# A hybrid decoder layer on one core: routing in another order, two embedding jobs moved behind the last expert, one expert's weights loaded earlier

## What is computed

```
x1 = LN1(alpha*x + merged @ w_o)
lg = x1 @ w_rg + b_rg ; g = argmax(lg)              # expert group
le = (x1 @ w_re + b_re)[group g] ; top 2, softmax    # two experts a token
y  = sum over the two: weight * (silu(x1 @ w_gate[e]) * (x1 @ w_up[e])) @ w_down[e]
x2 = LN2(alpha*x1 + y)
x3 = LN3(alpha*x2 + sigmoid(x2 @ w_ple_gate + b) * (p @ w_ple))
```

## Time and profile before

| | |
|---|---|
| three runs | 579.6 us median, 578.49 to 579.79 |
| profiled execution | 579.29 us, span 577.6 us, mean granted TensorE clock 0.971 |
| TensorE products | busy 534.0 us, 92% of the span |
| VectorE | 291.0 us, 50% |
| ScalarE | 189.5 us, 33% |
| GpSimd | 65.5 us, 11% |
| HBM read and written | 150.43 MB and 2.90 MB, 265 GB/s over the span |
| chain that ended last | TensorE 66%, VectorE 13%, DMA 11%, ScalarE 3% |

### The profile page before, as it was taken

How to read it: one execution, slowest core, us unless ns; L and a number is a source line. 1 busy time by engine, 2 the same in 40 slices (tenths; PEclk the granted TensorE clock), 3 DMA queues, 4 the chain that set the end, 5 groups by cost and what they waited for, 6 DMA issues and landing times.

```text
span 577.6 us, 9625 instructions
## 1 busy us (share of the span) xinstructions
PE 534.0 (92%) x3647; PEld 386.8 (67%) x3647; DVE 291.0 (50%) x633; ACT 189.5 (33%) x357; POOL 65.5 (11%) x92
## 2 busy tenths in 40 slices
PE   7899979999999879988999999999998899969992
PEld 7899868888889878777574544544544445446871
DVE  3442776565485567678453223222222222368878
ACT  4445444434355333052331111111111111246333
POOL 2000002322260640000000000000000000014010
PEclk9999989999999998977999999999999999979997
DMA  8996434875240980078399999999999999990101
GB/s 277 371 348 200 133 119 136 289 232 172 86 147 19 306 302 14 1 291 364 130 422 337 424 421 423 421 422 421 421 422 422 422 419 422 386 328 30 56 37 54
DMA packets 48796, 153.72 MB, mean 266 GB/s; under 512 B 3376, under 2 KB 28149, under 8 KB 36336
## 3 DMA queue, kind: packets, MB, share of 16 engines
q1 hardware_dynamic: 43778, 138.25, 62.6%
q0 software_dynamic: 3936, 12.60, 7.0%
q10 hardware_dynamic: 1046, 2.37, 1.2%
HBM read 150.43 MB, written 2.90 MB: 265 GB/s over the span
## 4 chain that ended last, share of the span: by engine, by line
PE 66%; DVE 13%; DMA 11%; ACT 3%; issue 2%; POOL 2%; SPq 1%; DVEq 1%; ACTq 0%; POOLq 0%
PE bank L1948 17%; PE bank L1629 16%; DMA ring<-in_w_up_dram 8%; PE bank L1961 7%; PE bank L1589 6%; DMA ring<-in_w_in_dram 3%; PE bank L1817 2%; PE bank L1970 2%; PE bank L2056 2%; PE bank L1892 2%; PE bank L1684 1%; PE bank L1954 1%; PE bank L1859 1%; ACT arena L699 1%; DVE arena L1174 1%
## 5 line engine op out<-in xcount | busy, mean ns | idle before, releaser
L1948 PE MATMUL bank<-ring,arena 128*64 128x256 f32 x1024 | 128.6, 392 | 5.2 <-DMA ring<-in_w_up_dram 2.6
L1948 PEld LDWEIGHTS bank<-ring,arena 128*64 128x64 f32 x1024 | 70.0, 134 | 60.1 <-issue 21.1
L1336 DVE TENSOR_TENSOR arena<-bank,arena 128x512 f32 x32 | 22.1, 692 | 133.5 <-PE bank L1970 127.7
L1629 PE MATMUL bank<-x_high,w_high 128*128 128x320 f32 x248 | 79.8, 322 | 2.3 <-ACT arena L661 2.3
L1629 PE MATMUL bank<-x_low,w_high 128*128 128x320 f32 x248 | 77.3, 312 | 0.0
L1629 PE MATMUL bank<-x_high,w_low 128*128 128x320 f32 x248 | 77.1, 311 | 0.0
L1961 PE MATMUL bank<-ring,arena 128*64 128x512 f32 x256 | 61.9, 604 | 0.0
L972 DVE TENSOR_TENSOR w_low<-ring,w_high 128x1024 fp32r<-128x1024 f32 x32 | 40.1, 1259 | 27.8 <-ACT w_high L643 27.7
L1629 PEld LDWEIGHTS bank<-x_high,w_high 128*128 128x128 f32 x248 | 47.2, 190 | 4.0 <-issue 3.9
L1629 PEld LDWEIGHTS bank<-x_low,w_high 128*128 128x128 f32 x248 | 47.2, 190 | 0.1
L1629 PEld LDWEIGHTS bank<-x_high,w_low 128*128 128x128 f32 x248 | 47.2, 190 | 0.0
(11 more groups left out here) (317 smaller groups left out, 887.3 us busy)
## 6 DMA issues: line engine op xcount, KB each, us to landing
ring<-in_w_gate_dram SPq DMA_DIRECT2D x32, 1024.0 KB, 16.2
ring<-in_w_up_dram SPq DMA_DIRECT2D x32, 1024.0 KB, 18.4
ring<-in_w_down_dram SPq DMA_DIRECT2D x32, 1024.0 KB, 18.9
ring<-in_w_in_dram SPq DMA_DIRECT2D x16, 1024.0 KB, 10.9
arena<-in_cache_k_dram POOLq DMA_DIRECT2D x16, 256.0 KB, 3.8
arena<-in_cache_v_dram POOLq DMA_DIRECT2D x16, 256.0 KB, 3.8
ring<-in_w_o_dram SPq DMA_DIRECT2D x4, 1024.0 KB, 11.3
ring<-in_w_ple_gate_dram SPq DMA_DIRECT2D x4, 1024.0 KB, 16.5
```

Source lines behind the costliest of these rows:

```text
L1336: V.tensor_tensor(YsT[:, :, bass.ds(place, WIN)].rearrange("p (d c) n -> p c d n", d=2), b[:, :].rearrange("p (c d n) -> p c d n", c=4, d= ...
L1629: last = mm(bank[j % 2][:, 0:T], w[:, j % 4, k, :], x[:, k, :], start=(k == n == 0), stop=(k == KD - 1 and n == 2))
L1948: last = mm(b[WIN * f:WIN * (f + 1), 0:256].rearrange("p (s n) -> p s n", s=2), x[:, WIN * k:WIN * (k + 1)], w[:, :, k, f, :], start=(k == ...
```

## The change

Four things are done, and they touch all engines' lists.

Loads: SyncE issues the third expert's gate and up (`load_pair(2)`) behind the first's and ahead of the second's. GpSimd issues `x_again`'s sample rows and `ln1_side[0]` behind the eight adds, not ahead of them.

Routing: the second tile is turned ahead of the first tile's routing products, the third tile ahead of the embeddings' turn. ScalarE copies both halves of the second tile (VectorE's copy falls away), and casts `x_part[0]` before. VectorE's `part_low(1)` is earlier; the last `x_part` is made in two halves, one on either side of the permutation. The products for offset and count go behind the gather, five products on `ones` stand in their old place, and VectorE picks the first window before it reads the offsets.

Embeddings: job two moves from the expert loop (which is one loop now, not two) to the routing, jobs three and four from ahead of the last four experts to behind the last turned result, in other banks.

Last result: `pairs(4)` stays ahead of the last `put`, `low_gate(0)` goes behind it, `low_gate(1)` to GpSimd, and `low_gate(2)` two steps earlier in the turning.

```diff
-        EMBED_BANKS = (3, 4, 6, 7, 6)
-        EMBED_FIRST = 2
+        EMBED_BANKS = (3, 4, 5, 0, 2)
+        EMBED_FIRST = 3
-        GATE_POOL = (3, 5, 7)
+        GATE_POOL = (1, 3, 5, 7)
@@ sync
             load_pair(0)
+            load_pair(2)
             for e in range(1, 5):
-                load_pair(e)
+                if e != 2:
+                    load_pair(e)
                 load_down(e - 1)
@@ gpsimd
             pool.dma_start(x_again[:, 0:2, :], xp_d).then_inc(x2_here, 16)
-            for h in range(2):
-                pool.dma_start(x_again[64 * h:64 * h + 64, 2, 0:512], xs_d[:, 512 * h:512 * (h + 1)]).then_inc(x2_here, 16)
-            load_sides(pool, ln1_side[0], a["ln1_g"][0], ln1_here)
...
                 pool.tensor_tensor(mT[:, n, :], gT[:, n, :], gT[:, 8 + n, :], ALU.add).then_inc(m_set, 1)
+            for h in range(2):
+                pool.dma_start(x_again[64 * h:64 * h + 64, 2, 0:512], xs_d[:, 512 * h:512 * (h + 1)]).then_inc(x2_here, 16)
+            load_sides(pool, ln1_side[0], a["ln1_g"][0], ln1_here)
@@ scalar
             norm(2)
+            part_high(0)
+            act.wait_ge(x1t_ps, 3)
+            nc.scalar.copy(x1T[:, 0:4, P:2 * P], four(bank[2], P)).then_inc(x1t_a, 1)
+            norm(3)
             columns(x1T, 1, x1t_ps, x1t_a)
-            part_high(0)
-            norm(3)
+            part_high(1)
+            columns(x1T, 2, x1t_ps, x1t_a)
...
-            columns(x1T, 2, x1t_ps, x1t_a)
-            part_high(1)
...
             result_out(main, EXPERTS)
+            for j in range(3, 5):
+                embedding_out(j)
@@ vector
-            columns(x1T, 1, x1t_ps, x1t_v)
             norm1(2)
-            columns(x1T, 2, x1t_ps, x1t_v)
...
             part_low(0)
+            columns(x1T, 2, x1t_ps, x1t_v)
+            part_low(1)
...
-            part_low(1)
+            dve.wait_ge(high_set, TILES)
+            last_part_low(0)
...
             permutation(0)
...
+            last_part_low(1).then_inc(low_set, 1)
-            dve.wait_ge(rank_ps, 2)
...
             pick(0, 0, main["xg"])
+            dve.wait_ge(rank_ps, 2)
+            link(V.tensor_scalar(near_f[:, :], off[:, 1:1 + NEAR], 320.0 - WIN, None, ALU.min))
+            link(V.tensor_copy(near_i[:, :], near_f[:, :]))
+            second = near(1)
             pick(1, second, main["xg"])
...
-            for n in range(2):
-                low_gate(n)
+            pairs(4)
             put(main, EXPERTS, bank[4 + 1], last_place)
...
+            low_gate(0)
             for g in range(10):
...
-                if g == 7:
+                if g == 5:
                     low_gate(2)
@@ tensor
             pe.wait_ge(wr_here, 32)
+            turn_tile(x1, 1, x1t_ps, x1_set)
             for t in range(TILES):
                 if t == 2:
+                    turn_tile(x1, t, x1t_ps, x1_set)
                     turn_embeddings()
-                if t > 0:
-                    turn_tile(x1, t, x1t_ps, x1_set)
-                pe.wait_ge(x1t_v, t + 1)
-                pe.wait_ge(x1t_a, t + 1)
+                pe.wait_ge(x1t_v, (1, 1, 2)[t])
+                pe.wait_ge(x1t_a, (1, 3, 4)[t])
...
             embedding(1)
+            embedding(2)
...
+            idle_products(5, bank[6])
...
-            with pe.Fori(0, 3) as i:
-                four_experts(i * 4 + 5, list(range(RING)), in_turn(i * 16 + 16))
-            embedding(2)
-            with pe.Fori(3, EARLY // 4 - 1) as i:
+            with pe.Fori(0, EARLY // 4 - 1) as i:
                 four_experts(i * 4 + 5, list(range(RING)), in_turn(i * 16 + 16))
-            embedding(3)
-            pe.wait_ge(pe_out, 3)
-            embedding(4)
...
             turn_result(main, EXPERTS, bank[5])
+            embedding(3)
+            embedding(4)
```

More of the change, by code:

```diff
@@ L873, in _ @@
                 result_out(main, n)
-            with act.Fori(0, 3) as i:
+            with act.Fori(0, EARLY // 4 - 1) as i:
                 four_experts(i * 4 + 5)
-            embedding_out(2)
-            with act.Fori(3, EARLY // 4 - 1) as i:
-                four_experts(i * 4 + 5)
-            for j in range(3, 5):
-                embedding_out(j)
             act.wait_ge(starts_set, 1)
@@ L1223, in part_low, with last_part_low @@
                 V.tensor_tensor(in_groups(x_part[2 + t][:, :]), grouped(x1[:, t, :]), in_groups(x_part[t][:, :].bitcast(F32)), ALU.subtract).then_inc(low_set, 1)
+            def last_part_low(h):
+                r, other = slice(64 * h, 64 * h + 64), slice(64 - 64 * h, P - 64 * h)
+                return V.tensor_tensor(in_groups(x_part[4][other, :])[:, :, r], grouped(x1[r, 2, 0:512]), in_groups(x_part[4][r, :].bitcast(F32))[:, :, r], ALU.subtract)
             dve.wait_ge(stored, 16 * 7)
             part_low(0)
+            columns(x1T, 2, x1t_ps, x1t_v)
+            part_low(1)
             def over_last(v, n):
@@ L1310, in _ @@
             permutation(0)
-            dve.wait_ge(high_set, TILES)
-            for h in range(2):
-                r, other = slice(64 * h, 64 * h + 64), slice(64 - 64 * h, P - 64 * h)
-                last = V.tensor_tensor(in_groups(x_part[4][other, :])[:, :, r], grouped(x1[r, 2, 0:512]), in_groups(x_part[4][r, :].bitcast(F32))[:, :, r], ALU.subtract)
-            last.then_inc(low_set, 1)
-            dve.wait_ge(rank_ps, 2)
+            last_part_low(1).then_inc(low_set, 1)
             off = bank[6][:, 128:160]
-            link(V.tensor_scalar(near_f[:, :], off[:, 1:1 + NEAR], 320.0 - WIN, None, ALU.min))
-            link(V.tensor_copy(near_i[:, :], near_f[:, :]))
             def pick(b, place, done):
@@ L1345, in near @@
                 return dve.value_load(near_i[0:1, e - 1:e], min_val=0, max_val=320 - WIN)
-            second = near(1)
             dve.wait_ge(pads_set, 1)
@@ L1415, in four_experts @@
                         pairs(j)
-                    if pairs_too and j == 3:
-                        pairs(4)
             first_experts()
@@ L1586, in by_parts @@
                             else:
-                                pe.wait_ge(wl_set, Z_JOBS + KD + 4 + (3, 5)[hf])
-                                pe.wait_ge(pads_set, 1 + (1, 3)[hf])
+                                pe.wait_ge(wl_set, Z_JOBS + KD + 4 + (2, 4)[hf])
+                                pe.wait_ge(pads_set, 1 + (2, 4)[hf])
                         last = mm(b[0:x.shape[1], 256 * q0:256 * q1].rearrange("p (s n) -> p s n", n=256), x,
@@ L1591, in by_parts, with idle_products @@
                 return last
-            def idle_products(n):
+            def idle_products(n, b=bank[7]):
                 for _ in range(n):
-                    mm(bank[7][:, 0:P], ones[:, :], ones[:, :], start=True, stop=True)
+                    mm(b[:, 0:P], ones[:, :], ones[:, :], start=True, stop=True)
             pe.wait_ge(ones_set, 1)
@@ L1882, in _ @@
             starts(2, False, True).then_inc(rank_ps, 1)
-            for o, X in ((128, GG), (160, Mt)):
-                for u in range(TILES):
-                    last = mm(bank[6][:, o:o + 32], ones[0:ROWS[u], :], X[0:ROWS[u], u, :], start=(u == 0), stop=(u == TILES - 1))
-            last.then_inc(rank_ps, 1)
+            idle_products(5, bank[6])
             def gather(j, parts, t):
@@ L1914, in _ @@
                 gather_all(j)
+            for o, X in ((128, GG), (160, Mt)):
+                for u in range(TILES):
+                    last = mm(bank[6][:, o:o + 32], ones[0:ROWS[u], :], X[0:ROWS[u], u, :], start=(u == 0), stop=(u == TILES - 1))
+            last.then_inc(rank_ps, 1)
             def other_half():
@@ L1932, in spread_places @@
             def spread_places():
-                pe.wait_ge(pe_out, 5)
                 for b, pos in ((bank[6], pos1), (bank[7], pos2)):
@@ L2025, in _ @@
             turn_result(main, EXPERTS, bank[5])
+            embedding(3)
+            embedding(4)
             with pe.If(crowded > 0):
                 pe.wait_ge(main["out"], EXPERTS)
+                pe.wait_ge(pe_out, 5)
                 pe.sem_inc(over["freed"], 1)
```

## The result

The changed kernel takes 573.24 us at the median of seven runs (571.82 to 576.61), before 579.6 us (578.49 to 579.79). The ratio taken over all runs is 0.9903, 95% interval 0.9877 to 0.993: faster by 1.0% (1.1% by the medians alone), against a forecast of 573.6. The profiled execution has a span of 573.9 us, where the kernel before had 577.6. It is one of the longer executions (575.55 us), so the profiles differ by 3.7 us where the medians differ by 6.4.

What follows compares the result with a forecast made beforehand. The DMA queue was taken as the slow partner, its restart set by the first expert, so an earlier first expert brings the end forward. Terms -1.6 - 2.1 - 1.0 - 1.0 = -5.7 took 579.3 to 573.6 us; range 571.0 to 577.5.

Steps and rivals of the forecast that it cites:

- A: Branch stage: GpSimd's adds begin earlier once four loads move behind them, removing TensorE's 1.60 us rest; -1.6 us.
- Load order: Third expert's loads issued earlier: slots fill sooner, but were already full before the first expert starts; 0 us.
- B: Routing to first expert: gather at full clock, offset products moved behind it, first expert at 276.8, not 278.88; -2.1 us.
- The step on the clock: Routing: third embedding and five constant products ahead of the gather keep it at full clock, 25 products taking 3.8 us.
- C: Last four experts: without embeddings ahead they follow the loads' 7.47 us pace, last expert at 495.7, not 496.76; -1.0 us.
- D: Behind the last expert: embeddings fill TensorE's rest, turning starts unmoved but at full clock, gw_low pieces move; -1.0 us.
- rival 4: Turning of the last result: clock falls despite the embeddings ahead, so D gives 0; 574.6 us, chance 0.12.
- the likeliest case: Whole kernel: the forecast's own case, chance 0.54, spanning 571.5 (embeddings at full clock, D at its bound) to 575 us.
- The sign of being wrong: First expert not at least 3 us earlier, or experts' end pace below 7.4 with a wait for another engine.

Runs made afterwards that it cites:

- best: Changed kernel with embedding three in place of the five constant products, four and five products' kin aside: embeddings three and four mid-loop, six constant products before the turning; 569.37 us.
- p_routing: Kernel before with the routing part alone, embeddings three and four left ahead of the last four experts; 577.03 us, ratio 0.9959.
- p_pool: Kernel before with only the four small GpSimd loads issued behind the eight adds; 576.55 us, ratio 0.9941.
- p_tail: Kernel before with the end alone: embeddings three and four behind the last turned result, gw_low pieces away from ahead of the last put; 577.0 us, ratio 0.9955.
- whole_again: The changed kernel run once more without any edit, beside three variants on one chip; 572.2 us, ratio 0.9884.
- mid_cold: Changed kernel with embeddings three and four in the middle of the expert loop and nothing in their old place; 572.48 us, ratio 0.9884.
- mid_idle: Changed kernel with embeddings three and four in the middle of the expert loop, six products on a constant in their old place; 572.08 us, ratio 0.9871.
- p_order: Kernel before with only the third expert's gate and up issued behind the first's, ahead of the second's; 578.02 us, ratio 0.9989.
- off_ahead: Changed kernel with the six offset products back ahead of the gather, in place of the five products on a constant; 573.25 us, ratio 0.9898.

## Why the prediction was right

*A.* Forecast -1.6, measured -1.83 (33.59 to 31.76). The bound, TensorE's one rest, was a little small: the stage shrank by 0.2 more than that rest. What I didn't see is in the next column: the ten kernels with this edit have a projection of 33.0 us on average, the four without it 32.1. What sets this column is the stretch at half clock (last section). Whether the edit sets that stretch stays open: one kernel on each side breaks the pattern (best 32.04, p_routing 33.12), and if half of A were given back there, p_pool would not have gained 2.7 by its medians.

*Load order.* Forecast 0. Neither run tells it from 0; a gain of up to 1.7 us isn't excluded.

*B.* Forecast -2.1; 30.89 to 28.47, -2.4 against the profile of before, and -1.9 against the mean of the four kernels with the old routing (30.34). The profile of before is the longest of the four, so -1.9 is the better size. Inside the sum two items were off and cancelled: the third routing group starts 0.9 earlier, not 0.4, and three embeddings took 7.53, not 6.88. The step on the clock held: the five products are worth 1.4 of the gain.

*C.* Forecast -1.0. It is -1.13 in p_tail and whole_again. In the first profile of the changed kernel it is only -0.55, in the main because its last expert waited 1.11 for the ring, where the other kernels with this end waited about 0.7.

*D.* Forecast -1.0, measured -1.0 in p_tail, the changed kernel and whole_again, and -0.9 against the mean of the four kernels with the old end. Two items were off. The turning was to start where it did; it starts 0.3 earlier behind the last expert (15.0 us, before 15.35), so the clock and the moved pieces gave 0.7. And the argument on the page was a wrong reading: I took the rise in the old trace as one behind transposes alone, but there too the combining products had begun first. The kernel before, timeline and window:

```profile
516.25 0.77 PE L2056 MATMUL bank<-yj_high,Pj 128*128 128x512 f32 x1
```

```profile
516.00:518.00 2.00, 2.00 (x11) 1.64 (x10) 1.39 (x2) 1.73 (x3) 0.00 (x0) 0.78 1.03 253
```

In mid_cold the fall comes right behind a group of transposes, and the rise only after combining products had begun at 508.71. What the Trainium skill says, page "TensorE: Matmul & The Clock Gate" (Part 4: PE-mode transpose), that transposes don't count as busy, agrees with that fall; but TensorE also rested 1.61 us ahead of that group and 0.96 behind it, and no run separates the two. What failed is the consequence I drew from it as rival 4: behind the embeddings the clock stayed at 1.00 through the whole turning.

*The sum.* By columns -1.83 - 2.42 - 1.13 - 1.01 = -6.4 in whole_again, forecast -5.7; the medians moved by 6.4 and 7.1. That the first median lies within 0.4 us of the forecast is in part luck, since the columns moved 0.7 further than forecast. The low end given for the likeliest case, 571.5, does not follow from its own parts, which give 572.0 (embeddings at full clock 1.0 more, D at its bound 0.6 more). Outside the terms, the stretch from first to sixth last expert is 0.7 shorter in the ten kernels with the new routing (178.81 on average, 179.53 in the four without). The traces put it where the loads take up again after their second pause, at about 305: from 308 to 314 the four moved 306 to 389 GB/s and the ten 412 to 430. Which edit does it I have not found.

*The sign of being wrong.* The prediction named one: the first expert not at least 3 us earlier. In the profile of the changed kernel it starts at 277.62, only 1.3 earlier than 278.88. The sign was badly chosen, since it counts from the span's start, and that execution reached its branch stage 2.0 us later and had a projection 1.0 us longer. By the two columns that belong to the change, branch and routing, the first expert is 4.25 us nearer, and in whole_again it starts 3.8 earlier.

## What to carry over

When a kernel's end follows one early event (here the first expert, which restarts the loads), cut every profile at the same rows and compare stretches, and look first at how far each stretch varies where nothing was changed: 1 us shows in those that repeat, where single executions of the changed kernel lie 3 to 5 us apart (571.39 to 574.43, 571.82 to 576.61). A rest filled with useful work is only free if the next step was not waiting to start in it; here the embeddings in TensorE's last rest held the turning back by 1.9 us, and they were free in the middle of the loop, since TensorE catches up with the loads behind them and waits for `ring` before the loop's end all the same (at 447.28 in mid_idle, at 441.25 in the changed kernel). Work that only keeps the clock up has to be tried: five products on a constant did it, six offset products in the same place did not.

## What the runs showed of the hardware

The same instructions took 181.00 to 184.63 us to the branch stage, and 30.94 to 33.25 in the projection, where the clock stood at 0.50 for a shorter or longer time. In the changed kernel's profile, the first row of the projection and two windows:

```profile
216.06 0.55 PE L1590 MATMUL bank<-wo_high,m_high 128*128 128x256 f32 x1 [3.31 <-DVE m_low L1136]
```

```profile
216.00:220.00 4.00, 3.94 (x18) 3.97 (x19) 4.00 (x2) 4.00 (x3) 1.92 (x4) 0.50 0.99 363
220.00:224.00 4.00, 4.00 (x29) 4.00 (x28) 4.00 (x3) 2.04 (x2) 0.00 (x0) 0.77 0.77 197
```

TensorE is busy without a pause there and still at 1.2 GHz; ahead of it stood one rest of 3.31 us. The same rest of 3.31 us stands there in the kernel before and in p_order. Their windows, before first:

```profile
216.00:220.00 4.00, 4.00 (x22) 4.00 (x23) 4.00 (x2) 4.00 (x3) 0.04 (x1) 0.57 0.18 66
```

```profile
216.00:220.00 4.00, 3.85 (x33) 3.65 (x32) 4.00 (x3) 3.98 (x3) 0.00 (x0) 1.00 0.74 274
```

Added up from such windows over the projection, the time at half clock is 0 us in p_order (30.94), 3.4 in before, p_tail and best (32.04 to 32.14), and 5.5 to 6.1 in the other ten (33.00 to 33.25). So the projection's spread is that of the time at half clock. Up to the branch stage it goes the same way, less strictly: at 1.00 throughout in p_order (181.00, the shortest), and some 10 us at half clock in the three longest (183.22, 184.30 and 184.63). Why one execution has more of it than another no run shows.

In off_ahead the clock fell in the middle of work without a rest of its own:

```profile
266.00:268.00 2.00, 1.90 (x12) 1.67 (x12) 1.86 (x6) 0.00 (x0) 0.00 (x0) 0.78 0.07 21
268.00:270.00 2.00, 2.00 (x9) 2.00 (x9) 1.90 (x5) 0.00 (x0) 0.00 (x0) 0.50 0.00 0
```
